# A four-stage transformer kernel: norms between stages by PSUM bank, with the first weight units split in the stage ahead

## The reference, cut to what matters

```python
def rms_norm(x, g):
    xf = x.astype(jnp.float32)
    y = xf * lax.rsqrt(jnp.mean(xf * xf, -1, keepdims=True) + EPS)     # EPS = 1e-6
    return (y * g.astype(jnp.float32)).astype(x.dtype)

for i in range(2):                       # mixer 0: latent attention (MLA), mixer 1: differential attention
    a = mixer_i(rms_norm(h, norm_g[i, 0]))
    h = h + rms_norm(a, norm_g[i, 1])
    f = conv_ffn(rms_norm(h, norm_g[i, 2]))            # up 1024 -> 2*2816, 3-tap conv, gelu gate, down
    h = h + rms_norm(f, norm_g[i, 3])
...
# third block: h += 0.5*swiglu(norm(h)); h += sparse attention and a gated linear recurrence; h += 0.5*swiglu(norm(h)); final norm
```

## Time and profile before

| quantity | value |
|---|---|
| median of 3 runs | 1211.7 us (1211.58, 1211.7, 1215.43) |
| the profiled execution, its own time | 1215.52 us |
| its span, first to last instruction | 1213.6 us |
| mean granted clock of TensorE | 0.991 |
| busy share of the span | PE 96%, PEld 82%, DVE 67%, ACT 57%, POOL 5% |
| DMA | 194.55 MB, 160 GB/s over the span |

### The profile page before, as it was taken

How to read it: one execution, slowest core, us unless ns; L and a number is a source line. 1 busy time by engine, 2 the same in 40 slices (tenths; PEclk the granted TensorE clock), 3 DMA queues, 4 the chain that set the end, 5 groups by cost and what they waited for, 6 DMA issues and landing times.

```text
span 1213.6 us, 19122 instructions
## 1 busy us (share of the span) xinstructions
PE 1170.0 (96%) x6627; PEld 990.7 (82%) x6641; DVE 809.6 (67%) x1169; ACT 695.9 (57%) x1175; POOL 66.4 (5%) x98
## 2 busy tenths in 40 slices
PE   9999999999899989999999999999988999999997
PEld 7976788888799867888886888887887877888885
DVE  5855788887656558888878555556656655665554
ACT  5455666665556547666656554545565545555543
POOL 0201000000200020000002000000000220000000
PEclk9999999999899999999999999999999999999999
DMA  7514666666343436666654666644674015767661
GB/s 225 180 56 125 184 204 191 195 175 203 111 140 132 148 115 179 203 182 203 184 163 139 207 184 181 205 122 131 184 236 139 1 36 168 200 175 201 182 165 60
DMA packets 241056, 194.55 MB, mean 160 GB/s; under 512 B 11214, under 2 KB 223792, under 8 KB 241008
## 3 DMA queue, kind: packets, MB, share of 16 engines
q1 hardware_dynamic: 240928, 193.88, 53.4%
q10 hardware_dynamic: 80, 0.03, 0.0%
HBM read 192.84 MB, written 1.05 MB: 160 GB/s over the span
## 4 chain that ended last, share of the span: by engine, by line
PE 85%; DVE 6%; ACT 4%; DMA 2%; issue 1%; POOL 1%; SPq 1%; POOLq 0%; ACTq 0%; DVEq 0%
PE psum L601 26%; PE psum L602 13%; PE psum L595 12%; PE psum L596 12%; PE psum L597 12%; DVE lo_u L1701 1%; PE psum L1178 1%; DMA raw_u<-in_cmp_v_w 1%; ACT hi_u L1273 1%; ACT hi_u L1276 1%; DVE lo_u L1718 1%; DMA raw_u<-in_diff_w_qkv 1%; PE psum L937 1%; PE psum L1150 1%; DVE normed L1735 1%
## 5 line engine op out<-in xcount | busy, mean ns | idle before, releaser
L601 PE MATMUL psum<-act_hl,hi_u 128*128 128x512 f32 x1392 | 495.9, 399 | 4.5 <-DVE lo_u L1718 3.2
L602 PE MATMUL psum<-act_hl,lo_u 128*128 128x256 f32 x1392 | 390.3, 280 | 0.0
L601 PEld LDWEIGHTS psum<-act_hl,hi_u 128*128 128x128 f32 x1392 | 261.5, 188 | 70.8 <-issue 7.1
L1718 DVE TENSOR_TENSOR lo_u<-raw_u,hi_u 128x2048 fp32r<-128x2048 f32 x109 | 249.8, 2291 | 93.6 <-ACT hi_u L1276 57.5
L602 PEld LDWEIGHTS psum<-act_hl,lo_u 128*128 128x128 f32 x1392 | 262.8, 189 | 3.1
L1346 ACT ACTIVATE arena<-psum 128x256 f32<-128x256 f32 x174 | 66.1, 380 | 166.9 <-PE psum L602 166.8
L1783 DVE TENSOR_TENSOR arena<-psum,arena 128x256 f32<-128x256 f32 x174 | 73.6, 423 | 110.2 <-ACT arena L1346 110.0
L1282 ACT ACTIVATE hi_u<-raw_u 128x2048 fp32r<-128x2048 f32 x72 | 137.3, 1907 | 8.5 <-DMA raw_u<-in_ffn_w_gu 8.5
L595 PE MATMUL psum<-hi_d,hid_hi 128*128 128x512 f32 (+1 forms) x352 | 138.8, 394 | 0.1
L596 PE MATMUL psum<-lo_d,hid_hi 128*128 128x512 f32 (+1 forms) x352 | 137.9, 392 | 0.0
L597 PE MATMUL psum<-hi_d,hid_lo 128*128 128x512 f32 (+1 forms) x352 | 137.0, 389 | 0.0
(11 more groups left out here) (249 smaller groups left out, 1673.7 us busy)
## 6 DMA issues: line engine op xcount, KB each, us to landing
raw_u<-in_ffn_w_up SPq DMA_DIRECT2D x88, 512.0 KB, 5.6
raw_d<-in_ffn_w_down SPq DMA_DIRECT2D x86, 512.0 KB, 3.6
raw_u<-in_ffn_w_gu SPq DMA_DIRECT2D x84, 512.0 KB, 5.6
raw_u<-in_diff_w_qkv SPq DMA_DIRECT2D x24, 512.0 KB, 4.6
raw_u<-in_w_in SPq DMA_DIRECT2D x24, 512.0 KB, 4.3
raw_u<-in_mla_w_o SPq DMA_DIRECT2D x8, 512.0 KB, 3.7
raw_u<-in_diff_w_o SPq DMA_DIRECT2D x8, 512.0 KB, 3.7
raw_u<-in_w_out SPq DMA_DIRECT2D x8, 512.0 KB, 4.1
```

The source lines that it names most:

```text
L601: pe.matmul(psum[0:n, bank, :], s_hi, m_hl.rearrange("p a t -> p (a t)"), start=start, stop=False)
L602: return pe.matmul(psum[0:n, bank, SEQ:], s_lo, m_hl[:, 0, :], start=False, stop=stop)
L1718: dve.tensor_tensor(v[0], v[1], v[2].bitcast(F32), ALU.subtract).then_inc(S("lo_u_done"), 1)
```

## The change

1. **Banks.** PE raises `bank_done` behind the last matmul of banks 0, 1 and 2; bank 3 has the stage's own last semaphore. ACT's squares and DVE's gain products in a `post` are per bank (512 columns). For the second token half the addition to `resid` and the next norm's squares are in two halves of 512 too.
2. **eps and the mean.** `Square` gets `scale = 1/32`, so that its sum is the mean. In the posts eps is added by ACT in an `Identity` on one column, which serves as the bias of a second one that joins the two bank sums. In the next norm, a 1025th column of `resid` holds a constant whose scaled square is eps. POOL keeps only the power.
3. **Who scales.** For the second token half, DVE writes columns 0 to 639 of `normed` and ACT columns 640 to 1023.
4. **First units.** Unit `FIRST` of a stage is split inside the stage ahead: behind MLPs, on ACT and DVE in tile 20 in place of nothing (`t < 21`); behind mixers, at the mixer's end. Its load and that of `SECOND` are moved ahead on SP, past nine table loads and a gain in the DIFF seam. `SECOND` is split in halves: behind MLPs ACT splits it at the MLP's end and between the posts (`split_part`), DVE one half within the post or the addition and one behind `act_lo`; elsewhere ACT splits it between and behind the eight `act_hi`.
5. **Filler.** `WARM` goes from (19, 3, 1) to (16, 2, 1) and from (12, 3, 1) to (6, 2, 1); the first norm keeps its own.

```diff
-WARM = [(0, 4, 6)] + 4 * [(19, 3, 1)] + 2 * [(12, 3, 1)]
+WARM = [(0, 4, 6)] + 4 * [(16, 2, 1)] + 2 * [(6, 2, 1)]
+BEHIND_FFN = [N_DIFF, N_F2, N_MIX]
+MIDDLE = 5 * P
...  # SP, end of an MLP: the next stage's first two units around the last down load
+                for load in following[:1]:
+                    load()
                 load_down(f, FT - 1, 1, width(f, FT - 1))
+                for load in following[1:]:
+                    load()
...
-            ffn(0)
+            ffn(0, 0, [lambda: load_unit(U_QK), lambda: load_unit(U_QK + 1)])
...  # POOL
+            def mean_root(name, t, ready, count):
+                v = st[:, ST_OF[name], t:t + 1]
+                pool.wait_ge(S(ready), count)
+                pool.tensor_tensor(v, v, half[:, 0:1], ALU.pow).then_inc(S("rstd"), 1)
...  # ACT, a post
+                for t in range(TT):
+                    for c in range(2):
+                        n = 4 * POST_OF[i] + 2 * t + c + 1
+                        bank_ready(i, 2 * t + c)
+                        act.activation(junk[:, c * BANK:c * BANK + BANK], psum[:, 2 * t + c, :], ACT.Square,
+                                       scale=1 / ROOT_D, accum_out=s[:, 4 + c:5 + c]).then_inc(S("post_sums"), 1)
+                        act.wait_ge(S("post_sums"), n)
+                        if c == 0:
+                            act.activation(s[:, 6:7], s[:, 4:5], ACT.Identity, bias=eps[:]).then_inc(S("post_halves"), 1)
+                        else:
+                            act.wait_ge(S("post_halves"), 2 * POST_OF[i] + t + 1)
+                            act.activation(s[:, t:t + 1], s[:, 5:6], ACT.Identity, bias=s[:, 6:7])\
+                                .then_inc(S("post_means"), 1)
+                    if t == 0 and i in BEHIND_FFN:
+                        split_part(SECOND[i], 1)
...  # ACT, the norm's squares of token half 1
+                    for c, (c0, c1) in enumerate(((0, BANK), (BANK, D + 1))):
+                        act.wait_ge(S("resid_ready"), 3 * (i - 1) + 2 + c)
+                        act.activation(junk_eps[:, c0:c1], resid_eps[:, t, c0:c1], ACT.Square, scale=1 / ROOT_D,
+                                       accum_out=s[:, 4 + c:5 + c]).then_inc(S("row_sums"), 1)
+                    act.wait_ge(S("row_sums"), 2 * i)
+                    act.activation(s[:, 1:2], s[:, 5:6], ACT.Identity, bias=s[:, 4:5]).then_inc(S("row_means"), 1)
...
+                act.activation(normed[:, 1, MIDDLE:], resid[:, 1, MIDDLE:], ACT.Copy,
+                               scale=st[:, ST_OF[f"norm{i}"], 1:2]).then_inc(S("normed_rest"), 1)
...  # ACT and DVE, an MLP's tile 20
-                    elif t < 20:
+                    elif t < 21:
                         split_u(u + 2)
...  # DVE, a post
+                for t in range(TT):
+                    for c in range(2):
+                        w = slice(c * BANK, c * BANK + BANK)
+                        dve.wait_ge(S("post_sums"), 4 * j + 2 * t + c + 1)
+                        dve.tensor_tensor(normed[:, t, w], psum[:, 2 * t + c, :], gain_row[:, j % 2, w], ALU.mult)\
+                            .then_inc(S("post_gained"), 1)
+                    if t == 0 and i in BEHIND_FFN:
+                        split_half(SECOND[i], 0)
+                    dve.wait_ge(S("post_gained"), 4 * j + 2 * t + 2)
+                    dve.wait_ge(S("rstd"), root_no(f"post{j}", t))
+                    for w in (slice(0, BANK), slice(BANK, D)) if t else (slice(0, D),):
+                        dve.scalar_tensor_tensor(resid[:, t, w], normed[:, t, w], st[:, ST_OF[f"post{j}"], t:t + 1],
+                                                 resid[:, t, w], ALU.mult, ALU.add).then_inc(S("resid_ready"), 1)
```

More of the change, by code:

```diff
@@ L507, in _ @@
             pool.memset(half[:], -0.5).then_inc(S("half_set"), 1)
+            pool.memset(eps[:], EPS).then_inc(S("eps_set"), 1)
             pool.wait_ge(S("half_set"), 1)
@@ L1322, in norm @@
                         split_u(SECOND[i])
-            def post_sums(j, halves, whole, n):
-                for t, (name, count) in enumerate(((halves, j // 2 + 1), (whole, n))):
-                    act.wait_ge(S(name), count)
-                    act.activation(junk[:].rearrange("p (a b) -> p a b", a=2), psum[:, 2 * t:2 * t + 2, :], ACT.Square,
-                                   accum_out=st[:, ST_OF[f"post{j}"], t:t + 1]).then_inc(S("post_sums"), 1)
-                    act.wait_ge(S("post_sums"), 2 * j + t + 1)
+                    if i in (N_F0, N_F1, N_F3) and k in (3, 7):
+                        split_part(SECOND[i], k // 4)
             def ffn(f):
@@ L1748, in norm @@
                                              ALU.subtract).then_inc(S("act_lo"), 1)
[L1749 removed]
+                    if i == N_MLA and k == 3:
                         split_u(SECOND[i])
[L1752 to L1764 removed]
@@ L1766, in add @@
-            def add(factor, waits):
-                two = lambda v: v.rearrange("p (a b) -> p a b", a=2)
-                for t in range(TT):
-                    dve.wait_ge(S(waits[t][0]), waits[t][1])
-                    dve.scalar_tensor_tensor(two(resid[:, t, :]), psum[:, 2 * t:2 * t + 2, :], factor,
-                                             two(resid[:, t, :]), ALU.mult, ALU.add).then_inc(S("resid_ready"), 1)
+                if i in BEHIND_FFN:
+                    split_half(SECOND[i], 1)
+                elif i != N_MLA:
+                    split_u(SECOND[i])
@@ L1917, in mla @@
                         split_u(U_UKV + 3)
-                for i in range(2):
+                for i in range(3):
                     split_u(U_MO + i + 2)
```

163 lines of the change are left out of this document (105 added, 58 removed).

## The result

| | before | changed |
|---|---|---|
| median, us (4 runs each, same chip) | 1213.01 (1211.58 to 1215.43) | 1205.84 (1204.5 to 1206.62) |
| ratio, 95% interval | | 0.9935 [0.9923, 0.9948] |
| profiled execution, us | 1215.5 | 1206.07 |
| its span, us | 1213.6 | 1204.3 |

The change makes the kernel faster, by 7.2 us in the medians and 9.3 in the profiled spans. I had said 1202.4, which is 3.4 too low. The range 1198 to 1208 held; the forecast's own range, 1199 to 1205.5, was missed by 0.3. The median of before, with one run more, is 1213.0 and not the 1211.7 that I started from, so against 9.3 us forecast on the median stand 7.2. Against the profiled execution I had taken 12.4 off and 9.3 went.

What follows compares the result with a forecast made beforehand. PE, busy 96%, bounds the kernel, and its gaps at the seams are serial chains. Terms -3.4 -2.1 +0 -1.4 -1.6 -1.0 +0.2 = -9.3 us took 1211.7 to 1202.4; own range 1199 to 1205.5, wider range 1198 to 1208.

Steps and rivals of the forecast that it cites:

- F0 and F1: Seams from the attention stages into MLP 0 and MLP 1: shorter serial chain, 1.7 us saved each, 3.4 in both.
- MIX: Seam from MLP 2 into the mixer stage: old gap 6.70 us, new 5.25, forecast -1.4 us.
- rival (e): On ACT: the change doesn't do what it says, through a table load for `Identity`; judged no case, no chance given.
- MLP ends: Tile 20 of MLP 0 and 1: DVE's added halves delay `lo_d`, so PE waits 1.0 us more in each.
- DIFF: Seam from MLP 0 into the differential stage: 11.4 to 8.3 us, 3.1 saved; -2.1 net of the MLP wait.
- F2: Seam from MLP 1 into MLP 2: gap 9.2 + 0.75 to 8.3 + 0.7 us; 0 net of the MLP wait.
- F3: Seam from the mixer stage into MLP 3: old gap 6.13 us, new product at 4.5, forecast -1.6 us.
- The clock: Behind the MLP 0 seam: granted clock kept, 3.1 us off the profiled execution; median runs taken to have kept it already.
- (a): Rival, seams behind MLP 0 and 1: the clock is lost at both; 1205.5 or 1208.6 us; chance 0.18.
- (b): Rival, seams: extra small steps and semaphores cost some 5 us, half of the seam gain; 1207 us; chance 0.15.
- (c): Rival, four seams: POOL's power gets between DVE's two half additions, holding the second 0.5 us; 1204.4 us; chance 0.08.
- (d): Rival, five seams: shorter filler costs the clock, 3.1 us each, +15.5 against -9.3; 1218 us; chance 0.05.

Runs made afterwards that it cites:

- e6: Changed kernel with squares and gamma products of the product norms over two banks at once again; ratio to before 0.9944.
- e7: Changed kernel with the residual addition and squares of token half 1 whole again, not in halves; ratio to before 0.9958.
- e1: Changed kernel plus one tiny ScalarE square ahead of the wait for x, so the table load comes early; ratio to before 0.9919.
- e5: Changed kernel with four more filler matmuls ahead of the first norm's first transposes, table load left late; ratio to before 0.9940.
- e8: Changed kernel with VectorE's two subtractions for the next stage's first unit behind the MLP's last tile, not inside tile 20; ratio to before 0.9921.
- r1: The kernel before, unchanged, run once more for a second profile; one run, 1214.23 us.
- e9: Kernel before with 31 filler matmuls in place of 19, and 4 in place of 3, in the seam behind MLP 0; ratio to before 0.9999.
- e4: Changed kernel with the differential stage's first two weight units loaded at their old place, the split staying in tile 20; ratio to before 1.0046.
- e3: Changed kernel with half of the next stage's first unit split behind the addition of token half 0 at the mixer's end; ratio to before 0.9941.
- c1: Changed kernel with the edits of e1, e3 and e8 together; ratio to before 0.9910.
- c2: c1 with the second unit's first half split behind the scaling of token half 1 in the seams behind MLP 0 and 1; 1200.26 us, ratio to before 0.9889.

## Why the forecast was right, and where it wasn't

**Right, with its reasons.** F0 and F1 (-1.7, measured -1.73 and -1.74), MIX (-1.4, -1.50), the end (-1.0, -0.97). Part of the agreement is luck: the old seams read 0.22 us too short for want of one filler record, and the new ones came out up to 0.2 longer than forecast (7.69 against 7.5 in F0, 5.42 against 5.25 in MIX), and the two errors cancel. e6 shows that the banks carry part of F0 and F1 (0.42), e7 that in MIX and at the end 0.7 us each is the addition by bank, and that the halved addition I counted in F0 and F1 gives at most 0.09: the rest there is the POOL operation that left and the shared scaling, by the chain's arithmetic; those two weren't tried alone.

**The term that failed is the start: +0.2 taken, +2.26 measured.** I priced the ScalarE part and looked no further. Against rival (e) I counted the table loads, 12 and 12, but not what each waits for. e1 (2.07 back with the load early) and e5 (1.2 back with the clock kept) show it.

**MLP ends: +1.0 each, measured +0.53 and +0.69.** The mechanism is right (e8 takes 0.46 and 0.41 back). The size isn't: behind tile 20's hidden product at 291.70, `lo_d` starts 2.61 us later, and 1.86 before (291.19 to 293.05), so it is 0.75 late and not 0.97, and e8's 0.18 us of PE's 0.74 us wait stay without the subtractions.

**DIFF: -3.1 measured as -3.20, but on a lucky execution of before.** The load never held ACT, as I said. In r1 and e9 before's seam is 13.3 and 13.0: there the same change is worth 4.6 to 4.9. How much of it is the split of `FIRST` that left the seam was not run alone: e6 gives 0.7 of it to the banks, and e4, which loads late again, moves the wait into tile 20 and leaves the seam at 8.38. F2: 0 forecast, 8.83 + 0.69 against 10.17, so -0.65; the seam gave more (1.34) and the MLP took less.

**F3: -1.6, measured -0.78.** 0.1 to 0.4 us is the subtraction that the change put in front of the addition (e3). The rest is my chain, where I took the early end at each step: addition done at +0.7, squares 1.5, power 2.35, scaling 2.9 behind the stage's end. In e3 they are done at 1.0, 1.9, 2.8 and 3.5 (its DVE row 1005.17 above and the steps behind it), and the product follows at 5.20.

**The clock: -3.1 on the profiled execution.** The DIFF stage gave 2.71: 1.6 of it is the dip near 430 that comes and goes, and the other 1.1 what the dip of the earlier trace rows still cost behind the first product (in r1 it lay ahead of that product, and the stage took 122.27). On the median my choice was that before's runs had kept the clock; e9 says that it hardly matters there. One more line of the gap between forecast and profile, 0.96, is the mixer stage: it ran between 175.96 us (e8) and 179.14 (e1) on nearly the same code. The dips near 875 and 935 don't explain all of that (none in e8, one in e6 with 175.97, one in c1 with 178.16); PE's waits there for `lo_u`, the weights' low parts (L1775 in the changed kernel), go from 5.2 us (e6) to 7.2 (c2, 178.53). Why was not tried.

**Rivals.** (a) fell: the clock is 1.00 in DIFF and F2, PE idle for 1.18 and 1.17 us before their first transposes. (b) fell on the 0.29 us rows. (c) fell: 1.42 us for both additions in F0. The rule of the Trainium skill (SBUF — State Buffer, Who interferes with whom), which the page gives for DVE's two-port modes while these additions have two inputs in SBUF, was open at this point; here the addition, which had started first, went on, and POOL was the one that waited (0.78 in place of 0.56), as the rule has it; but it was not held to the end of the second addition. (d) fell in the seams, with six fillers in MIX and F3 at clock 1.00, and the clock fell in one place that I had not looked at, the start, where the filler is not shorter: there the wait grew. (e) fell as I wrote it and stood in another form.
